# Compressed scores of both key heads in one step, and the router's transposed columns in two small buffers

## The reference

```python
# per key head h (2 of them), per query head j of that key head (4), per query
s = (q @ kc.T)                      # 31 scores
s = where(allowed, s, -1e30)        # -> ck("cneg")
p = exp(0.125 * (s - max(s))) * allowed01      # -> ck("c01")
p = p / max(sum(p), 1e-20) * gate   # gate of (query, head, compressed branch)
out += p @ vc
```

## Time and profile before

| what | us |
|---|---|
| median of 3 runs | 2460.68 |
| lowest and highest | 2452.25 and 2461.19 |
| the profiled execution, its own time | 2447.28 |
| its span, first to last instruction | 2445.4 |
| TensorE busy (share of the span) | 2226.5 (91%) |
| VectorE busy | 612.2 (25%) |
| ScalarE busy | 323.1 (13%) |
| GpSimd busy | 206.8 (8%) |

### The profile page before, as it was taken

The page is one execution under the profiler, slowest core; times in us unless marked ns, Lnnn a source line. Parts: engine busy times, 40 slices in busy tenths (PEclk is TensorE's granted clock), DMA queues, the critical chain, the costliest instruction groups (busy, mean ns, idle before and its releaser), DMA issues.

```text
span 2445.4 us, 20383 instructions
## 1 busy us (share of the span) xinstructions
PE 2226.5 (91%) x8284; PEld 1022.6 (42%) x8284; DVE 612.2 (25%) x1311; ACT 323.1 (13%) x652; POOL 206.8 (8%) x186
## 2 busy tenths in 40 slices
PE   8999999999999999999999999988888888877886
PEld 4554444445444444466644463333323333322332
DVE  2246544311633210033431142111111111111114
ACT  2014424202111100021110120000000000000001
POOL 0001111010344200000000001000000000000001
PEclk9999999999999999998999999998999999999998
DMA  6201010322232321219422339999999999999995
GB/s 273 86 35 69 35 69 4 151 103 78 95 118 79 141 77 72 101 52 161 155 102 83 159 156 408 426 426 426 425 426 426 426 427 427 425 425 422 421 426 221
DMA packets 69759, 552.43 MB, mean 226 GB/s; under 512 B 21656, under 2 KB 26392, under 8 KB 37600
## 3 DMA queue, kind: packets, MB, share of 16 engines
q1 hardware_dynamic: 42384, 515.49, 51.8%
q10 hardware_dynamic: 17200, 23.23, 3.2%
q0 software_dynamic: 10080, 12.38, 1.4%
HBM read 543.91 MB, written 35.68 MB: 237 GB/s over the span
## 4 chain that ended last, share of the span: by engine, by line
PE 69%; DMA 26%; DVE 3%; ACT 1%; issue 1%; DVEq 0%; POOL 0%; SPq 0%; ACTq 0%; POOLq 0%
PE ps L380 25%; DMA sb<-in_eu 12%; PE ps L1008 9%; PE ps L456 8%; DMA sb<-in_eg 8%; PE ps L698 8%; PE ps L1040 4%; DMA sb<-in_ed 4%; PE ps L399 2%; PE ps L856 2%; PE ps L628 2%; PE ps L541 1%; PE ps L574 1%; PE ps L568 1%; DMA sb<-in_mgg 1%
## 5 line engine op out<-in xcount | busy, mean ns | idle before, releaser
L380 PE MATMUL ps<-sb 128*128 128x512 f32 (+2 forms) x1536 | 613.8, 559 | 2.8 <-issue 1.4
L1008 PE MATMUL ps<-sb 128*64 128x512 f32 x2048 | 487.7, 632 | 108.6 <-DMA sb<-in_eu 79.3
L380 PEld LDWEIGHTS ps<-sb 128*128 128x128 f32 x1536 | 279.7, 190 | 315.9 <-issue 312.6
L1008 PEld LDWEIGHTS ps<-sb 128*64 128x64 f32 x2048 | 176.7, 145 | 398.8 <-issue 398.7
L1040 PE MATMUL ps<-sb 128*64 128x512 f32 x992 | 232.5, 623 | 26.9 <-ACT sb L1427 17.2
L456 PE MATMUL ps<-sb 128*128 128x512 f32 x512 | 236.1, 600 | 0.3 <-DMA sb<-in_mgg 0.3
L698 PE MATMUL ps<-sb 128*128 128x512 f32 x448 | 192.5, 592 | 0.7 <-ACT sb L1247 0.7
L1451 DVE TENSOR_TENSOR sb<-sb 128x32 f32<-128x32 f32 (+10 forms) x292 | 115.4, 412 | 115.7 <-PE ps L662 66.2
L1040 PEld LDWEIGHTS ps<-sb 128*64 128x64 f32 x992 | 73.7, 143 | 164.2 <-issue 137.6
L456 PEld LDWEIGHTS ps<-sb 128*128 128x128 f32 x512 | 91.3, 190 | 100.0 <-issue 98.9
L698 PEld LDWEIGHTS ps<-sb 128*128 128x128 f32 x448 | 85.0, 190 | 107.6 <-issue 107.6
(11 more groups left out here) (283 smaller groups left out, 1481.5 us busy)
## 6 DMA issues: line engine op xcount, KB each, us to landing
sb<-in_eg SPq DMA_DIRECT2D x64, 2048.0 KB, 33.6
sb<-in_eu SPq DMA_DIRECT2D x63, 2048.0 KB, 33.9
sb<-in_ed SPq DMA_DIRECT2D x63, 2048.0 KB, 32.4
sb<-in_m SPq DMA_DIRECT2D x16, 2048.0 KB, 7.4
sb<-in_mg SPq DMA_DIRECT2D x8, 1536.0 KB, 6.9
sb<-in_winF SPq DMA_DIRECT2D x5, 2048.0 KB, 7.3
sb<-in_mgg SPq DMA_DIRECT2D x4, 2048.0 KB, 8.0
sb<-in_wo SPq DMA_DIRECT2D x4, 2048.0 KB, 7.3
```

Source lines behind the costliest of these rows:

```text
L380: ins = pe.matmul(out, lhsT, rhs, start=k == 0, stop=k == len(pieces) - 1)
L1008: ins = pe.matmul(o[64 * e:64 * e + 64, :], x[:, k, 64 * e:64 * e + 64], weight(2 * mat + e)[:, 512 * k:512 * k + 512], start=k == 0, stop ...
```

## The change

Three edits stand in the diff.

*Compressed scores.* A tile is now one block of queries with both heads. TensorE's four pairs of matmuls alternate between the heads, three steps of the recurrence follow, then all eight transposes behind one wait, then one more step. VectorE adds the mask head by head and runs the rest of its chain once over 128x248 instead of twice over 128x124; its stream has two steps of the recurrence between the subtraction and the wait for the exponential. ScalarE takes one exponential of 128x248. The number of steps of the recurrence is unchanged, 16.

*Router's columns.* The transposed rows go to `HB[i % 2]`, which are the two `XG` buffers seen as 8x128, and no longer to `H`. From the third block on, the copies wait for the logits two blocks earlier. GpSimd's clearing of `XG` waits for the last logits.

*Ring.* Slot 8 (`H`) moves from the eighth place of the ring to the fifth. `ex 4` goes there and waits for the last `mg2` tile that reads `H`; `ex 5`, `ex 6` and `ex 7` go to slots 3, 0 and 5.

```diff
+        HB = [view(a, 0, 8, 128) for a in XG]
...
-        RING = [6, 1, 2, 4, 3, 0, 5, 8, 7]
+        RING = [6, 1, 2, 4, 8, 3, 0, 5, 7]
...
                 for i in range(4):
+                    o = [open_tile(pe, ("cs", i, h), 2 + h) for h in range(2)]
+                    for j in range(4):
+                        for h in range(2):
+                            ins = pe.matmul(o[h][:, 31 * j:31 * j + 31], qT[64 * h:64 * h + 64, j, 128 * i:128 * i + 128],
+                                            kcT[64 * h:64 * h + 64, :], start=True, stop=True)
+                            if j == 3:
+                                ins.then_inc(T.f("cs", i, h), 1)
+                    yield 3
+                    s3 = view(CT[i], 0, 8, 31)
                     for h in range(2):
-                        o = open_tile(pe, ("cs", i, h), 2 + h)
+                        o = open_tile(pe, ("ct", i, h), 4 + h)
+                        pe.wait_ge(S("cprob"), i + 1)
                         for j in range(4):
-                            ins = pe.matmul(o[:, 31 * j:31 * j + 31], qT[64 * h:64 * h + 64, j, 128 * i:128 * i + 128],
-                                            kcT[64 * h:64 * h + 64, :], start=True, stop=True)
-                        ins.then_inc(T.f("cs", i, h), 1)
-                        yield 2
-                        o = open_tile(pe, ("ct", i, h), 4 + h)
-                        pe.wait_ge(S("cprob"), 2 * i + h + 1)
-                        s3 = view(CT[(2 * i + h) % 4], 0, 4, 31)
-                        for j in range(4):
-                            ins = pe.transpose(o[0:31, 128 * j:128 * j + 128], s3[:, j, :], ident)
+                            ins = pe.transpose(o[0:31, 128 * j:128 * j + 128], s3[:, 4 * h + j, :], ident)
                         ins.then_inc(T.f("ct", i, h), 1)
+                    yield 1
...
-                    ins = pe.matmul(T.ap("lg", i)[:, 0:72], H[:, k, 128 * i:128 * i + 128], rw[:, k, :], start=k == 0, stop=k == 7)
+                    ins = pe.matmul(T.ap("lg", i)[:, 0:72], HB[i % 2][:, k, :], rw[:, k, :], start=k == 0, stop=k == 7)
...
                 for i in range(4):
-                    for h in range(2):
-                        n = 2 * i + h
-                        s3 = view(CT[n % 4], 0, 4, 31)
-                        act.wait_ge(S("csub"), n + 1)
-                        act.activation(s3, s3, ACT.Exp, scale=0.125).then_inc(S("cexp"), 1)
-                        yield 2
-                        if h == 0:
-                            copy(("ct", i, 0), PCT[0:31, :, 128 * i:128 * i + 128],
-                                 T.ap("ct", i, 0)[0:31, :].rearrange("p (a b) -> p a b", a=4))
+                    s3 = view(CT[i], 0, 8, 31)
+                    yield 1
+                    act.wait_ge(S("csub"), i + 1)
+                    act.activation(s3, s3, ACT.Exp, scale=0.125).then_inc(S("cexp"), 1)
+                    yield 2
+                    copy(("ct", i, 0), PCT[0:31, :, 128 * i:128 * i + 128],
+                         T.ap("ct", i, 0)[0:31, :].rearrange("p (a b) -> p a b", a=4))
+                    yield 1
...
-                copy(("xr2", i, 0), H[:, 0:4, 128 * i:128 * i + 128], T.ap("xr2", i, 0).rearrange("p (a b) -> p a b", a=4))
+                if i > 1:
+                    act.wait_ge(*T.full("lg", i - 2))
+                copy(("xr2", i, 0), HB[i % 2][:, 0:4, :], T.ap("xr2", i, 0).rearrange("p (a b) -> p a b", a=4))
...
                 for i in range(4):
+                    s3, st = view(CT[i], 0, 8, 31), CT[i][:, 248:256]
                     for h in range(2):
-                        n = 2 * i + h
-                        s3, st = view(CT[n % 4], 0, 4, 31), CT[n % 4][:, 124:128]
                         dve.wait_ge(*T.full("cs", i, h))
-                        if n > 3:
-                            dve.wait_ge(*T.full("ct", (n - 4) // 2, h))
-                        dve.tensor_tensor(s3, T.ap("cs", i, h)[:, 0:124].rearrange("p (j n) -> p j n", j=4),
+                        dve.tensor_tensor(s3[:, 4 * h:4 * h + 4, :], T.ap("cs", i, h)[:, 0:124].rearrange("p (j n) -> p j n", j=4),
                                           bc(ck("cneg")[:, 31 * i:31 * i + 31], 1, 4), ALU.add).then_inc(T.s("cs", i, h), 1)
+                    for h in range(2):
                         dve.wait_ge(*T.free("cs", i, h))
...
+                    after(own(dve.tensor_reduce(st, s3, op=ALU.max, axis=AX.X)))
+                    dve.tensor_tensor(s3, s3, bc(st, 2, 31), ALU.subtract).then_inc(S("csub"), 1)
+                    yield 2
+                    dve.wait_ge(S("cexp"), i + 1)
+                    after(tt(s3, s3, bc(ck("c01")[:, 31 * i:31 * i + 31], 1, 8), ALU.mult))
+                    after(own(dve.tensor_reduce(st, s3, op=ALU.add, axis=AX.X)))
+                    after(ts(st, st, 1e-20, None, ALU.max))
+                    after(own(dve.reciprocal(st, st)))
...
+                    dve.tensor_tensor(s3, s3, bc(st, 2, 31), ALU.mult).then_inc(S("cprob"), 1)
+                    yield 1
+                    copy(("ct", i, 1), PCT[32:63, :, 128 * i:128 * i + 128],
+                         T.ap("ct", i, 1)[0:31, :].rearrange("p (a b) -> p a b", a=4))
+                    yield 1
...
-            pool.wait_ge(S("mg2"), 8)
+            pool.wait_ge(*T.full("lg", 3))
...
-                if n == 6:
+                if n == 4:
+                    sp.wait_ge(*T.full("mg2", 7, 1))
+                if n == 7:
                     sp.wait_ge(*T.full("wo2", 3, 1))
-                if n == 7:
-                    sp.wait_ge(*T.full("lg", 3))
```

More of the change, by code:

```diff
@@ L1400, in scalar_program @@
                 half_square(0)
-                copy(("xr2", i, 0), H[:, 0:4, 128 * i:128 * i + 128], T.ap("xr2", i, 0).rearrange("p (a b) -> p a b", a=4))
+                if i > 1:
+                    act.wait_ge(*T.full("lg", i - 2))
+                copy(("xr2", i, 0), HB[i % 2][:, 0:4, :], T.ap("xr2", i, 0).rearrange("p (a b) -> p a b", a=4))
                 half_square(1)
-                copy(("xr2", i, 2), H[:, 6:8, 128 * i:128 * i + 128], T.ap("xr2", i, 2)[:, 0:256].rearrange("p (a b) -> p a b", a=2))
+                copy(("xr2", i, 2), HB[i % 2][:, 6:8, :], T.ap("xr2", i, 2)[:, 0:256].rearrange("p (a b) -> p a b", a=2))
                 act.wait_ge(S("block_v"), 4 + i + 1)
@@ L1626, in cmp_scores @@
                                           bc(ck("cneg")[:, 31 * i:31 * i + 31], 1, 4), ALU.add).then_inc(T.s("cs", i, h), 1)
+                    for h in range(2):
                         dve.wait_ge(*T.free("cs", i, h))
-                        after(own(dve.tensor_reduce(st, s3, op=ALU.max, axis=AX.X)))
-                        dve.tensor_tensor(s3, s3, bc(st, 2, 31), ALU.subtract).then_inc(S("csub"), 1)
-                        dve.wait_ge(S("cexp"), n + 1)
-                        after(tt(s3, s3, bc(ck("c01")[:, 31 * i:31 * i + 31], 1, 4), ALU.mult))
@@ L1632, in cmp_scores @@
-                        after(own(dve.tensor_reduce(st, s3, op=ALU.add, axis=AX.X)))
-                        after(ts(st, st, 1e-20, None, ALU.max))
-                        after(own(dve.reciprocal(st, st)))
-                        if n == 0:
-                            dve.wait_ge(S("gate"), 1)
-                        gcol = gate[:, i, :].rearrange("p (hd c) -> p hd c", c=3)[:, 4 * h:4 * h + 4, 0]
-                        after(tt(st, st, gcol, ALU.mult))
-                        dve.tensor_tensor(s3, s3, bc(st, 2, 31), ALU.mult).then_inc(S("cprob"), 1)
@@ L1640, in cmp_scores @@
-                        yield 2
-                        if h == 1:
-                            copy(("ct", i, 1), PCT[32:63, :, 128 * i:128 * i + 128],
-                                 T.ap("ct", i, 1)[0:31, :].rearrange("p (a b) -> p a b", a=4))
+                    after(own(dve.tensor_reduce(st, s3, op=ALU.max, axis=AX.X)))
+                    dve.tensor_tensor(s3, s3, bc(st, 2, 31), ALU.subtract).then_inc(S("csub"), 1)
+                    yield 2
+                    dve.wait_ge(S("cexp"), i + 1)
@@ new lines, in cmp_scores @@
+                    after(tt(s3, s3, bc(ck("c01")[:, 31 * i:31 * i + 31], 1, 8), ALU.mult))
+                    after(own(dve.tensor_reduce(st, s3, op=ALU.add, axis=AX.X)))
+                    after(ts(st, st, 1e-20, None, ALU.max))
+                    after(own(dve.reciprocal(st, st)))
+                    if i == 0:
+                        dve.wait_ge(S("gate"), 1)
+                    after(tt(st, st, gate[:, i, :].rearrange("p (hd c) -> p hd c", c=3)[:, :, 0], ALU.mult))
+                    dve.tensor_tensor(s3, s3, bc(st, 2, 31), ALU.mult).then_inc(S("cprob"), 1)
@@ L2016, in half_turn @@
                 dve.wait_ge(*T.full("xr2", i, 1))
-                dve.tensor_copy(H[:, 4:6, 128 * i:128 * i + 128],
+                if i > 1:
+                    dve.wait_ge(*T.full("lg", i - 2))
+                dve.tensor_copy(HB[i % 2][:, 4:6, :],
```

## The result

The first comparison gave 2439.14 us for the changed kernel (median of 7, 2434.42 to 2443.71) against 2452.25 for the kernel before (median of 7, 2447.95 to 2461.19): a ratio of 0.9943 with a 95% interval from 0.9926 to 0.996. Two further samples of the changed kernel gave 0.9963 (0.9945 to 0.9981) and 0.9962 (0.9945 to 0.9979). Over all executions of this study, 100 of the kernel before and 31 of the changed one, the means are 2451.65 and 2441.14 us, a difference of 10.5 (0.43%) with a standard error of 1.0. The forecast was a gain of 4.7.

A forecast was written before the change was run, and what follows sets the result against it. TensorE bounds the kernel before 1476.4 us, DMA the experts' stage after. Stalls -2.9, scores -1.3, rounding 0.5 make 4.7 us less, ring and router 0; set against the median 2460.68: 2456 us, range 2442 to 2463.

The forecast's parts named there:

- the price of a score call: Compressed scores on TensorE: 0.21 us a call, 1.7 us a block against 2.0, saving 1.3 us in all.
- Rival B: Compressed scores: alternation hides the weight loads, 2.5 us more gain than forecast, 2453.5 us; chance 0.15.
- The transposes: Compressed scores on TensorE: a block's eight transposes take 1.06 us, where four took 0.53.
- The 0.5 us of rounding: Scores' stage: 0.5 us of the 4.7 us gain put down to rounding in the cadences.
- The order worked through: Scores' stage, block by block: TensorE stalls 0.7 us at block 2 and 2.0 at block 3, 2.7 against 5.6.
- The chain: VectorE and ScalarE work between a block's scores and transposes: 3.96 us for both heads, against 2.85 for one.
- The ring: Experts' weight loads: moving one load earlier gains 0, as the queue had run dry; bounds 0 and -4.9 us.
- Rival A: Experts' stage from 1476.4 us: the moved load counts in full, 4.9 us shorter, 2451 us; chance 0.12.
- The router: Router's logits from another address and later XG clearing: 0; 1.9 us if the clearing blocked VectorE without cover.
- Rivals C: Compressed scores: alternating exposes a whole weight load, 0.19 us, in each call; +2.7 us, 2463 us; chance 0.08.
- D: Scores' stage: stalls only move; a chain of 5.2 us and no score gain leave under 1 us, 2460; chance 0.15.
- The base: Whole kernel: forecast set against the median, 2460.68 us, though the profiled execution took 2447.28, 13.4 below.

The follow-up runs named there:

- e5b: Kernel before, with only both heads' score matmuls of a block made together, alternating; chains and transposes stay per head: median 2445.33 us, ratio 0.9975.
- e3b: Changed kernel with the loop over heads outside the query heads, so score matmuls no longer alternate: median 2443.39 us, ratio 0.9965 to before.
- e4: Changed kernel with VectorE's two recurrence steps moved behind the scaling, so a block's chain runs whole: median 2440.43 us, ratio 0.9967 to before.
- f4: Changed kernel with a block's chain whole on VectorE and the xr2 convolution moved behind block 2's chain: median 2436.44 us, ratio 0.9938 to before.
- e2b: Kernel before with only the router's buffers and the ring as changed, compressed scores as before: median 2453.97 us, ratio 1.0017.
- f2: Kernel before with three unread 128x512 VectorE operations ahead of tile 20's chain, lengthening TensorE's wait there: median 2455.18 us, ratio 1.0012.

## Why the prediction was wrong

**The direction and the place were right, the size was too small.** Forecast: 4.7 us less, all of it in the scores' stage, nothing from the ring. Measured: 7.6 in that stage, nothing from the ring, 10.5 in the timed means.

**The step that failed is the price of a score call.** I took 0.21 us from L541, a row of two alternating calls in 0.42, and got -1.3. It measured 1.01 for eight, 0.13 a call, and -4.0: 2.7 of the 2.9 us that the stage gained beyond the forecast. The division by two was the error: in that row the two calls, one in each half, start 0.007 us apart and already run side by side, so 0.42 is the time of one call: 0.22 from the first record's start to the last's, and 0.20 from there to the next dense matmul. Eight calls are four such pairs, 0.81 from first to last start and the same 0.20. Rival B, to which I gave 0.15, had the right size, at its own bound of 0.13 a call. The rule of the Trainium skill ("TensorE: Matmul & The Clock Gate", Part 3), that a weight load overlaps a running matmul only when the row groups differ, gave 1.0 us a block, and the trace agrees with that time: 1.48 in head order and 1.01 alternating. What the trace shows is more than hidden loads: within a half the cadence stays at 0.11 a record, and whole calls of the two halves overlap. I had argued against the rule with the row of two, which in fact showed this overlap.

**The transposes I took at no gain.** It measured 0.8 us: rows of four cost 0.44 and not 0.53 when no scores follow, and the change put a step of the recurrence behind them (e5b has both).

**The 0.5 us of rounding in the forecast's sum has no row.** Nothing measured stands for it: 4.0, 0.8 and 2.8 make 7.6 without it. So the excess of 2.9 over the forecast is 2.7 of scores and 0.8 of transposes, less this 0.5 and 0.1 of waits.

**The order worked through was right.** I had no wait at blocks 0 and 1, 0.7 at block 2, 2.0 at block 3, and none at the attention's start; measured were none, none, 1.22, 1.58 and none, 2.8 against 2.7. That the total fits is in part luck, as the two waits miss by +0.5 and -0.4. Block 2 came out higher because the cheaper scores leave less cover ahead of the convolution's end; e3b, with dearer scores, has 0.75. The chain: 3.89 against 3.96. The causes of both waits were shown by e4 and f4.

**The ring was right**, and its proof too: a DMA queue at 0 GB/s before ex 8, 134.16 us from ex 0 to ex 9, and e2b no faster. I expected some 80 GB/s below 342 in the window before ex 8; it is 65 below (277). Rival A fell.

**The router was right.** `XG` is cleared from 1453.25 for 1.85 us beside `choose(3)`, and the interval from ex 0 to g(0) didn't move. VectorE's row after that reads the last rank; it still waited 1.84 us for TensorE, so `choose(3)` was done before:

```profile
1459.54 0.29 DVE L1456 TENSOR_TENSOR sb<-sb,ps 128x128 f32<-128x128 f32 x1 [1.84 <-PE ps L897]
```

The blocking that the Trainium skill, "SBUF — State Buffer", Who interferes with whom, describes is not seen: the operations of `choose(3)` run from 1453.31 to 1457.70, 4.39 us, against 4.40 before (1456.15 to 1460.55) without a clearing beside them. Few of them fall within the clearing's 1.85 us, one cast among them, so the trace says little about the rule itself.

**Rivals C and D fell**: a call costs 0.13 and not 0.44, and the waits halved.

**The base was the larger miss of the absolute time.** The forecast of 2456 hung on a median of three executions, 2460.68. The 100 executions have a median of 2451.6 and a range from 2440.2 to 2462.0. I saw that the profiled execution was 13 us below that median and kept the median all the same. Of the 17 us between 2456 and 2439, 9 are this, about 3 the score calls and transposes, 3 the excess that stays open, and the rest scatter. The profiled execution less the measured 7.6 would have been 2439.7, within 1 us of the three medians; with one execution as the base that would have been luck too.

## What to carry to other kernels

A load moved into idle time ahead of a stage that DMA bounds is worth nothing if that stage begins without a backlog, as here; where the next load waits for a slot that compute frees, the idle time just moves, and the place to look is the last microseconds before that slot. Short matmuls with K = 64 take half the time when those of the two halves of the partitions stand side by side in TensorE's order: join the rows and alternate. And before a row's time is divided by its calls, look in the trace whether they already overlap. And where a kernel's executions scatter by more than the change is worth, compare the length of the changed stretch in the traces and not the spans.

## What had not been expected of the hardware

Two K = 64 matmuls in different halves of the partitions start 0.007 us apart, and four in one half take as long (1.00 us) as eight over both (1.01). In head order the same eight take 1.48, because the second half starts 0.47 us late. Four transposes cost 0.44 us ahead of dense work and 0.53 ahead of K = 64 scores. And the clock: the same code from 104 to 120 us ran at 1.00 in nine traces and at 0.50 in five, where the way from its first matmul to the first score took 6.2 us longer in the changed kernel's trace (44.7 us after 38.5 before). Behind tile 01's wait of 1.11 us the clock stood at the lower level in f2 and at the full one in the kernel before and in e2b, which have the same wait.
